# Decay stage of a two-block model: gate rows turned once, and one 512-column product per unit instead of four 128-column ones

## The reference, cut to what matters

```python
        cs = jnp.cumsum(dtc * A, axis=1)
        Lm = jnp.exp(jnp.where(mask, cs[:, :, None] - cs[:, None, :], -jnp.inf))
        CB = jnp.einsum('btgn,bsgn->btsg', Cc, Bc)
        xdt = xc * dtc[..., None]
        y = jnp.einsum('btsg,btsge,bsgep->btgep', CB, Lm, xdt)
...
        a = jnp.where(mask, b[..., :, None] - b[..., None, :] + igc[..., None, :], -jnp.inf)
        w_intra = jnp.exp(a - m_t[..., None])
        qk = jnp.einsum('bhtd,bhsd->bhts', qc, kc).astype(F32) * w_intra
```

## Time and profile before

| | us |
|---|---|
| median of 3 runs | 2537.66 (2535.87 to 2540.64) |
| the profiled execution, its own time | 2538.27 |
| span of its trace | 2536.3 |
| TensorE busy | 2363.4 (93%) |
| VectorE busy | 1755.2 (69%) |
| ScalarE busy | 1322.4 (52%) |
| GpSimd busy | 594.9 (23%) |
| mean granted TensorE clock | 0.966 of full |

### The profile page before, as it was taken

How to read it: one execution, slowest core, us unless ns; L and a number is a source line. 1 busy time by engine, 2 the same in 40 slices (tenths; PEclk the granted TensorE clock), 3 DMA queues, 4 the chain that set the end, 5 groups by cost and what they waited for, 6 DMA issues and landing times. The chain is left out here.

```text
span 2536.3 us, 37032 instructions
## 1 busy us (share of the span) xinstructions
PE 2363.4 (93%) x14184; PEld 1975.0 (78%) x14184; DVE 1755.2 (69%) x2775; ACT 1322.4 (52%) x2660; POOL 594.9 (23%) x333
## 2 busy tenths in 40 slices
PE   8999988988999988978998899999999989999999
PEld 8866776767866766767786689998887866899987
DVE  1846757873856767867698679994257986799942
ACT  3457616763457617755746654443167476444431
POOL 3401305772401205762350010000034400100000
PEclk9999988998999988998998999999999989999999
DMA  4210029983200019982220213322231202133221
GB/s 164 89 34 18 4 83 354 356 309 114 88 34 18 16 61 356 360 293 106 79 87 1 78 54 103 115 99 93 70 110 67 84 1 92 35 121 111 100 83 67
DMA packets 54990, 285.80 MB, mean 113 GB/s; under 512 B 13216, under 2 KB 13216, under 8 KB 28704
## 3 DMA queue, kind: packets, MB, share of 16 engines
q1 hardware_dynamic: 45600, 266.65, 29.3%
q0 software_dynamic: 9216, 16.80, 1.7%
HBM read 275.02 MB, written 25.17 MB: 118 GB/s over the span
## 5 line engine op out<-in xcount | busy, mean ns | idle before, releaser
L253 POOL TENSOR_TENSOR weights_lo<-weights_raw,weights_hi 128x2048 fp32r<-128x2048 f32 (+4 forms) x49 | 221.3, 4516 | 677.9 <-POOLq L120 356.3
L264 PE MATMUL ps<-x_operands,weights_hi 128*128 128x256 f32 x1232 | 349.3, 284 | 7.4 <-DVE weights_lo L2054 6.8
L265 PE MATMUL ps<-x_operands,weights_hi 128*128 128x256 f32 x1232 | 347.0, 282 | 0.0
L266 PE MATMUL ps<-x_operands,weights_lo 128*128 128x256 f32 x1232 | 347.0, 282 | 0.0
L215 ACT ACTIVATE weights_hi<-weights_raw 128x2048 fp32r<-128x2048 f32 (+4 forms) x80 | 136.8, 1709 | 302.3 <-PE ps L266 287.6
L264 PEld LDWEIGHTS ps<-x_operands,weights_hi 128*128 128x128 f32 x1232 | 231.3, 188 | 10.1 <-DVE weights_lo L2054 9.8
L266 PEld LDWEIGHTS ps<-x_operands,weights_lo 128*128 128x128 f32 x1232 | 232.3, 189 | 0.0
L265 PEld LDWEIGHTS ps<-x_operands,weights_hi 128*128 128x128 f32 x1232 | 232.3, 189 | 0.0
L264 PE MATMUL ps<-weights_hi,attn_ht_hi 128*128 128x512 f32 (+2 forms) x576 | 203.6, 353 | 3.7 <-DVE weights_lo L253 2.2
L265 PE MATMUL ps<-weights_lo,attn_ht_hi 128*128 128x512 f32 (+2 forms) x576 | 200.3, 348 | 0.0
L266 PE MATMUL ps<-weights_hi,attn_ht_lo 128*128 128x512 f32 (+2 forms) x576 | 199.5, 346 | 0.0
(11 more groups left out here) (529 smaller groups left out, 6281.2 us busy)
## 6 DMA issues: line engine op xcount, KB each, us to landing
weights_raw<-in_stream SPq DMA_DIRECT2D x96, 1024.0 KB, 4.8
weights_raw<-in_expert_gu SPq DMA_DIRECT2D x34, 1024.0 KB, 9.4
expert_raw<-in_expert_gu SPq DMA_DIRECT2D x30, 1024.0 KB, 9.5
expert_raw<-in_expert_down SPq DMA_DIRECT2D x18, 1024.0 KB, 8.5
weights_raw<-in_expert_down SPq DMA_DIRECT2D x14, 1024.0 KB, 8.3
weights_raw<-in_stream SPq DMA_DIRECT2D x12, 960.0 KB, 4.7
ffn_raw<-in_stream SPq DMA_DIRECT2D x10, 1024.0 KB, 5.0
weights_raw<-in_stream SPq DMA_DIRECT2D x8, 700.0 KB, 8.5
```

The source lines that it names most:

```text
L253: eng.tensor_tensor(lo[:, 0:n], self.env.raw[:, u % self.RAW, 0:n], hi[:, 0:n].bitcast(F32), ALU.subtract).then_inc(self.lo_ready, 1)
L264: nc.tensor.matmul(out, a[0], b[0], start=start, stop=False, **more)
L265: nc.tensor.matmul(out, a[0], b[1], start=False, stop=False, **more)
L266: return nc.tensor.matmul(out, a[1], b[0], start=False, stop=stop, **more)
```

## The change

All 32 gate columns are written twice side by side (`decay_cols_twice`), and turned at the start of the stage by four transposes into 64 rows of 512 tokens in a bank. ScalarE rounds them to fp32r (`decay_rows`); VectorE then overwrites rows 32 to 63 with what the rounding lost. A unit's row is spread by one fp32r product over these 64 rows, whose stationary operand is one column of `decay_picks`, broadcast to 128, with a one at row k and a one at row k + 32. The first group's four products are split, two ahead of the first row and two behind the second. Some semaphores are merged under new names.

```diff
...
+    NR = 32
...
+        twice = local.enter_context(nc.sbuf_tensor("decay_cols_twice", [P, T, 2 * NR], F32, allow_name_mangling=True))
+        rows = local.enter_context(nc.sbuf_tensor("decay_rows", [2 * NR, S], F32R, allow_name_mangling=True))
+        picks = local.enter_context(nc.sbuf_tensor("decay_picks", [2 * NR, NR], F32R, allow_name_mangling=True))
+        turned = ps[0:2 * NR, 6, :]
...
             @block.tensor
             def _(pe):
+                def products(u, each, behind):
+                    for s in each:
+                        if behind is not None:
+                            pe.wait_ge(weighted, T * behind + s + 1)
+                        nc.tensor.matmul(ps[:, s, :].rearrange("p (t c) -> p t c", t=T), u["k"][:, s, :],
+                                         u["q"], start=True, stop=True).then_inc(products_ready, 1)
+
+                pe.wait_ge(cols_then_rows_lo, 1)
+                for t in range(T):
+                    last = nc.tensor.transpose(turned[:, t * P:(t + 1) * P], twice[:, t, :], ident)
+                last.then_inc(rows_turned, 1)
+                products(units[0], range(2), None)
+                pe.wait_ge(cols_then_rows_lo, 3)
                 for i in range(N + 2):
                     if i < N:
                         if i >= 2:
                             pe.wait_ge(gap_ready, T * (i - 1))
-                        for t in range(T):
-                            r = cols[:, t, units[i]["row"]:units[i]["row"] + 1].to_broadcast([P, P])
-                            last = nc.tensor.matmul(ps[:, 4 + i % 2, t * P:(t + 1) * P], r, ident, start=True, stop=True)
-                        last.then_inc(row_ready, 1)
-                    if 1 <= i <= N and new_group[i - 1]:
-                        u = units[i - 1]
-                        for s in range(T):
-                            if i > 1:
-                                pe.wait_ge(weighted, T * (i - 2) + s + 1)
-                            last = nc.tensor.matmul(ps[:, s, :].rearrange("p (t c) -> p t c", t=T), u["k"][:, s, :],
-                                                    u["q"], start=True, stop=True)
-                            last.then_inc(products_ready, 1)
+                        k = units[i]["row"]
+                        nc.tensor.matmul(ps[:, 4 + i % 2, :], picks[:, k:k + 1].to_broadcast([2 * NR, P]), rows[:, :],
+                                         start=True, stop=True).then_inc(row_ready, 1)
+                    if i == 1:
+                        products(units[0], range(2, T), None)
+                    elif 1 < i <= N and new_group[i - 1]:
+                        products(units[i - 1], range(T), i - 2)
...
             @block.vector
...
-                nc.vector.tensor_scalar(minus_cols[:, :, :], cols[:, :, :], -1.0, None, ALU.mult).then_inc(negated, 1)
+                nc.vector.tensor_tensor(picks[:, :], ident[0:2 * NR, 0:NR], ident[0:2 * NR, NR:2 * NR], ALU.add)
+                nc.vector.tensor_copy(twice[:, :, :].rearrange("p t (u c) -> p t u c", u=2),
+                                      cols[:, :, :].unsqueeze(2).to_broadcast([P, T, 2, NR])).then_inc(cols_then_rows_lo, 1)
+                nc.vector.tensor_scalar(minus_cols[:, :, :], cols[:, :, :], -1.0, None, ALU.mult).then_inc(cols_then_rows_lo, 1)
+                dve.wait_ge(rows_hi_then_floors, 1)
+                nc.vector.tensor_tensor(rows[NR:2 * NR, :], turned[NR:2 * NR, :], rows[NR:2 * NR, :].bitcast(F32),
+                                        ALU.subtract).then_inc(cols_then_rows_lo, 1)
...
             @block.scalar
             def _(act):
-                act.wait_ge(negated, 1)
+                act.wait_ge(rows_turned, 1)
+                nc.scalar.activation(rows[:, :], turned, ACT.Copy).then_inc(rows_hi_then_floors, 1)
+                act.wait_ge(cols_then_rows_lo, 2)
```

More of the change, by code:

```diff
@@ L1250, in decay_stage @@
     names = ("products_ready", "row_ready", "gap_ready", "exp_done", "weighted", "masked", "out_ready",
-             "out_stored", "negated", "floors_made", "values_ready", "vector_step")
-    (products_ready, row_ready, gap_ready, exp_done, weighted, masked, out_ready, out_stored, negated, floors_made,
-     values_ready, step) = (env.sem("decay", n) for n in names)
+             "out_stored", "cols_then_rows_lo", "rows_turned", "rows_hi_then_floors", "values_ready", "vector_step")
+    (products_ready, row_ready, gap_ready, exp_done, weighted, masked, out_ready, out_stored,
+     cols_then_rows_lo, rows_turned, rows_hi_then_floors, values_ready, step) = (env.sem("decay", n) for n in names)
+    NR = 32
     first_of_values = [u["group"][0] for u in units].index("m")
@@ L1332, in _ @@
                         if j == first_of_values:
-                            dve.wait_ge(floors_made, 1)
+                            dve.wait_ge(rows_hi_then_floors, 2)
                         dve.wait_ge(out_ready, j + 1)
@@ L1345, in _ @@
                     if i == 2:
-                        nc.scalar.activation(cols[:, :, 16:24], cols[:, :, 16:24], ACT.Exp, scale=-1.0).then_inc(floors_made, 1)
+                        nc.scalar.activation(cols[:, :, 16:24], cols[:, :, 16:24], ACT.Exp, scale=-1.0).then_inc(rows_hi_then_floors, 1)
                         values.copy(lambda out, x: nc.scalar.activation(out, x, ACT.Copy), 3).then_inc(values_ready, 1)
```

## The result

The changed kernel takes 2552.29 us (median of 5 runs, 2550.33 to 2556.05), the kernel before 2536.66 on the same chip (5 runs, 2535.06 to 2540.64). The ratio is 1.006, with a 95% interval of 1.0047 to 1.0073: **slower by 15.6 us**. The forecast was 2547, in the range 2531 to 2556.

The account below looks back on a forecast made before the run. The prediction took TensorE to bound the decay stage's mLSTM half, with ScalarE nearly as long per unit in the SSD half. Per stage 2.0 - 5.4 + 8.0 = +4.6, +9.2 in all, gave 2547 us, range 2531 to 2556.

Parts of the forecast that it names:

- What bounds the stage: Decay stage: TensorE bounds the mLSTM half; the stage's end moves with unit 13's value products.
- late start, at unit 3: Stage start: the chain ahead of the first row delays the first ReLU 2.5 us; 2.0 us lost per stage.
- rows 6 to 15: Where TensorE is the bound: cheaper row products gain 5.4 us per stage.
- clock: TensorE idles before the first value products, its clock falls to half until unit 4's group products; 8.0 us lost per stage.
- sum: Per decay stage: 2.0 - 5.4 + 8.0 = +4.6 us; +9.2 for both stages.
- six isolated rows: Among rows 6 to 15: each saves 0.43 us, a switch there and back included; 2.6 us together.
- four beside an mLSTM group's products: Among rows 6 to 15: the switch is already paid, so each saves 0.71 us; 2.8 us together.
- my rival with free switches: Row products: switches cost nothing, rows gain 7.1 us per stage; 2543.5 at half clock (0.10), 2527.5 if clock holds (0.05).
- length of the hole: TensorE idles 2.7 us before the first value products; were it 1 us shorter, the clock might hold.
- the clock holds: Rival: full clock through the decay stages, each 3.4 us shorter, 2531 us; chance 0.17.
- upper bound: Clock loss per stage is 10 us if the idle time ahead of the transposes brings half-clock time as well.

Follow-up runs that it names:

- lean fill: Changed kernel plus useless products only where TensorE would idle: before transposes, first value products, and those of units 2 and 14; 2531.98 us.
- kernels with 64 and 128 rows: Six old rows with the new row product on 64 array rows, 2529.3 us, and the same with 128 rows, 2531.49 us.
- six old rows: Changed kernel with rows 0 to 5 made by the old four products, transposes behind row 1, new product from row 6 on; 2529.3 us.
- kernel with 128 rows: Changed kernel with gate columns copied four times, so the row product uses 128 array rows instead of 64; 2545.07 us.
- the old rows: Changed kernel's start kept, but each row made by the old four 128-column products, turned rows made and not used; 2557.38 us.
- second execution: Traced execution from measuring the unaltered changed kernel again beside the lean fill; execution 2547.93 us, median of that set 2552.7 us.
- two old rows: Changed kernel with rows 0 and 1 made by the old four products, transposes behind them, new product from row 2 on; 2539.45 us.

## Why the prediction was right

**What bounds the stage.** Right. ScalarE's wait in the mLSTM half fell by the rows' gain, and the stage's end moved with unit 13's value products. From these to the end it takes 16.66 us in before and in every stage that ended at full clock.

**The terms,** for one stage, with the second stage of the changed kernel for the clock's term, since it has the one fall that I had priced:

| term | predicted | measured | from |
|---|---|---|---|
| late start, at unit 3 | +2.0 | +2.2 | lean fill 21.87, before 19.65 |
| rows 6 to 15 | -5.4 | -5.0 | unit 3 to 13: 41.50, before 46.45 |
| clock | +8.0 | +6.6 | 28.50, lean fill 21.87 |
| sum | +4.6 | +3.9 | 86.66, before 82.76 |

*Start.* The first ReLU came 3.54 us into that stage where I had 3.7. The transposes cost 0.46 us, not 0.94; the stage's first sum on VectorE took 0.41 and not 0.15. In the main the two errors cancel. The lean fill's own first ReLU stands at 3.78, so up to 0.2 us of this term could belong to the clock's.

*Rows.* From one unit's value products to the next, the six isolated rows save 0.21 to 0.43 us, 0.34 on the mean (3.13 apart before, 2.80 now, for one of them), where I had 0.43 for each; one of the dearest two (3.02 apart) waits 0.15 us for its masks. The four beside an mLSTM group's products save 0.61 to 0.84, 0.73 on the mean, and I had 0.71. The switch between 64 and 128 rows is real, 0.23 us between the kernels with 64 and 128 rows. The Trainium skill (TensorE: Matmul & The Clock Gate, "What overlaps and what doesn't") lets a weight load overlap products under way only if it goes to another group of rows. I took 64 rows among 128 for another group, though rows 0 to 63 belong to both. The runs disagree with that rule as it stands: with six old rows all products from 241.60 to 246.60 us use the same 128 rows, and TensorE is busy for 5.00 us with products and for 5.00 with loads at once. No kernel with 128 rows showed the 7.1 us of my rival with free switches: from unit 3 to unit 13 it gained 5.0, like the one with 64, as I read it because the switch had moved to the rows beside the mLSTM groups.

*Clock.* Right in place and length, near in price, and in cause only in part. In the first traced execution TensorE idles 2.63 us (I had 2.7) and the clock falls at 241.6 and 818.5, 1.0 us behind the start of the first value products. It is back at 258.7 and 835.5, within the second SSD group's products (I had 256 to 261). But I made the length of the hole decide: were it 1 us shorter, the clock might hold. The runs don't bear this out. The clock fell at the same place behind 1.69 us with the old rows, behind 0.64 us in one stage of the second execution, and, later in the stage (14.7 us into it), with two old rows behind holes of 0.55 and 0.45. The term was sized 1.4 us too high. The first value products ran at full clock for about a microsecond (3.65 us long, not 4.2), and a row lost 0.3 us, not 0.5. Value products of units 0 to 2, rows and group products lose 5.4, 0.9 and 1.7 us, together 8.0 where I had 9.3, and 1.4 of it comes off as waiting. The lean fill prices the rival "the clock holds": 2.6 us less per stage (I had 3.4), 2531.98 in all (I had 2531).

**What I left out.** The idle time ahead of the transposes (2.37 us; I had 2.2) gives a half-clock spell of its own in three of the four traced stages: 1.7, 1.3 and 1.6 us (first ReLU at 5.25, 4.83 and 5.17 against 3.54). I had it in the upper bound only. A second spell falls on the stage's end in two of four: unit 13 to end 18.50 and 16.94 us instead of 16.66, 1.8 and 0.3 lost. In the first traced stage that makes the whole difference: 86.66 + 1.7 + 1.8 = 90.2. The mean of the four stages is 88.4, so +5.6 per stage and 11.2 for both, where I had 9.2. The total is near the forecast in part by luck: a clock term too large, rows too small, two spells left out, and a remainder that no term of mine covers.

**What stays open.** The medians differ by 15.6 and 16.4 us, the stages by 11.2. Some 4 to 5 us are not located. One execution of each kernel is traced, and outside the stages the traced ones take between 2367 and 2376 us though that code is the same in all. Half clock in other places is likely a part of it. Of the kernel before, 68 launches stand beside the experiments. Their mean granted clocks are 0.964 to 0.969. Twice what is missing to 1, times the span, is the time at half clock: 167 us of a launch on the mean, and each us more of it goes with 0.4 us more of time (correlation 0.87). The changed kernel's two sets of launches (eleven in all) have 219 and 217 us. Its traced stages hold 44 to 48 of them, so 169 to 175 lie elsewhere, which by the 0.4 explains 1 to 3 us, an estimate. Why the clock is at half more often there, and the rest, stay open. Open too is what exactly brings a fall: each run tells how long TensorE idled and how busy it was, but none changes one without the other.

## What to carry to other kernels

Before work is taken off the engine whose clock is granted, ask for each place what it will wait for then: where another engine sets the pace, cheaper work only turns into waits, and here that went with 7 to 10 us at half clock per stage with two old rows, and with 17 to 27 where the start was late as well. Put the cheaper operation where the engine is the bound and leave the dear one where it has to wait anyhow (six old rows: 2529.3, 7.7 us better than before); a chain ahead of a stage belongs behind the first units, not in front of them. When pricing a change, look for full clock in the row of its own experiment, with useless products in the holes if need be, so that the gain of the operation and the loss of the clock are two numbers.

## What the hardware showed that I had not expected

- The clock fell without any long idle time: with two old rows TensorE was busy for 12.00 of the 13.00 us from 232 on and idled 0.55 us at most, and the clock still fell at 245.2. With six old rows, 12.91 of 13.00 us busy in the same part of the stage, it held. In the kernel before it held through an idle 1.69 us at the stage's start; with the late start and the old rows it fell 0.6 and 1.1 us behind 1.69 us of idle time ahead of unit 0's value products.
- Useless products pay where they keep the clock (2552.7 to 2531.98 us), and cost their full length where TensorE is the bound (0.7 us for three, units 3.49 apart and not 2.80).
- Four fp32 transposes of 128 columns took 0.44 to 0.50 us together, four products of the same size 0.94.
- Row products with a 64-row stationary operand cost 0.23 us more among 128-row neighbours than those with 128 rows (units 2.80 and 2.57 us apart).
